# A hybrid pooling and windowed-attention layer on eight cores: pooling on GpSimd, gates in token layout, crossbar transposes

## The reference, cut to what matters

```python
h = modulate(rms_norm(x, g_pre), shift, scale)                 # tokens x 1024, 4096 tokens a sample
xa, ga, q, k, v, gb, gm = split_columns(h @ w_in)              # 512 512 1024 256 256 1024 2048 columns
# branch A: per group of 128 channels, window w = 2, 4, 8, 16
pooled = mean(xa[t - w/2 : t + w/2]) - xa[t]                   # valid positions only
y_a = (pooled @ pool_w[g]) * pool_scale * silu(ga)
# branch B: each token attends to +-128 tokens, 256 context keys and a sink; 16 heads, 4 kv heads, rotary q and k
y_b = attention(q, k, v, k_ctx, v_ctx, sink) * silu(gb)
g = sigmoid(gm)
merged = g[:, :1024] * (y_a @ w_branch_a) + g[:, 1024:] * (y_b @ w_branch_b)
out = x + gate * rms_norm(merged @ w_out, g_post)
```

## Time and profile before

| | |
|---|---|
| time, median of 3 runs | 2472.1 us (2468.12 to 2604.85) |
| span of the profiled execution, slowest core | 2465.5 us |
| spans of the eight cores | 2454.4 to 2465.5 us |
| mean granted TensorE clock, by core | 0.989 to 0.992 |
| DMA, mean share of the 16 engines busy | about 0.15 after the first 200 us |

### The profile page before, as it was taken

One profiled execution on the slowest core, in us unless ns is written; L12 is line 12 of the kernel. 1 busy time (PEld: TensorE's weight loads), 2 busy tenths in 40 slices (PEclk: granted clock), 3 DMA queues, 4 the chain that ended last, 5 costly groups with the idle time before them and its releaser, 6 DMA issues.

```text
span 2465.5 us, 85698 instructions; the slowest of 8 cores (2454.4 to 2465.5 us)
## 1 busy us (share of the span) xinstructions
PE 2367.6 (96%) x34464; PEld 1821.1 (74%) x34464; DVE 1341.5 (54%) x3567; ACT 1225.7 (50%) x2375; POOL 678.0 (28%) x677
## 2 busy tenths in 40 slices
PE   6679999999999999999999999999999999999998
PEld 2447877787787787778777778777777877777776
DVE  1425555555555655555555555565555556556553
ACT  1324555555555555455544555555555555555453
POOL 1112232232323223223222232322322323232232
PEclk9889999999999999999999999999999999999999
DMA  8982111111111111111112111111111111111111
GB/s 220 188 157 66 49 49 55 40 58 47 41 58 49 47 49 49 56 40 61 61 40 66 47 40 58 49 48 48 49 56 40 58 47 40 58 49 49 39 39 44
DMA packets 44371, 148.35 MB, mean 60 GB/s; under 512 B 7376, under 2 KB 15696, under 8 KB 41424
## 3 DMA queue, kind: packets, MB, share of 16 engines
q1 hardware_dynamic: 41392, 121.18, 15.1%
q0 software_dynamic: 2592, 21.69, 5.0%
HBM read 126.79 MB, written 33.56 MB: 65 GB/s over the span
## 4 chain that ended last, share of the span: by engine, by line
PE 88%; DVE 3%; DMA 2%; POOL 2%; issue 2%; ACT 2%; another core or an unknown queue 1%; POOLq 0%; DVEq 0%; SPq 0%; ACTq 0%
PE pb L483 34%; PE pb L476 13%; PE pb L692 9%; PE pb L708 9%; PE pb L642 6%; PE pb L616 6%; PE pb L682 5%; DVE s_scr L723 2%; DMA s_W<-w_in 2%; PE pb L578 2%; ACT s_ttmp L711 2%; PE tb L659 1%; POOL s_small L718 1%; PE pb L340 1%; PE tb L460 1%
## 5 line engine op out<-in xcount | busy, mean ns | idle before, releaser
L483 PEld LDWEIGHTS pb<-s_hT,s_W 128*128 128x128 bf16 x15360 | 866.5, 98 | 145.9 <-issue 145.3
L483 PE MATMUL pb<-s_hT,s_W 128*128 128x128 bf16 x15360 | 937.2, 219 | 22.1 <-DVE s_scr L723 21.3
L619 ACT ACTIVATE s_PT<-pb 128x512 bf16<-128x512 f32 x1264 | 651.8, 603 | 271.9 <-PE pb L616 271.8
L476 PE MATMUL pb<-s_W,s_hT 128*128 128x512 bf16 (+1 forms) x2048 | 421.3, 354 | 2.4 <-DMA s_W<-w_in 2.4
L535 DVE TENSOR_TENSOR s_scr<-pb,s_ropet 128x512 f32<-128x512 f32 x256 | 164.9, 686 | 311.0 <-PE pb L483 310.7
L476 PEld LDWEIGHTS pb<-s_W,s_hT 128*128 128x128 bf16 x2048 | 192.8, 98 | 160.0 <-issue 6.0
L540 POOL TENSOR_TENSOR s_qT<-s_scr 128x512 bf16<-128x512 f32 x128 | 160.0, 1271 | 539.8 <-DVE s_scr L535 539.8
L696 POOL TENSOR_TENSOR s_mgT<-s_ub,s_scr 128x512 bf16<-128x512 f32 x128 | 162.4, 1269 | 404.8 <-DVE s_scr L673 404.8
L692 PE MATMUL pb<-s_ybT,s_wmf 128*128 128x128 bf16 x4096 | 249.6, 219 | 0.0
L651 DVE SCALAR_TENSOR_TENSOR s_yb<-pb,s_small,s_Gb 128x64 bf16<-128x64 f32 x1024 | 220.0, 277 | 29.1 <-DVE s_small L648 2.2
L708 PE MATMUL pb<-s_wmf,s_mgT 128*128 128x512 bf16 x1024 | 231.6, 379 | 1.5 <-POOL s_mgT L696 1.5
(11 more groups left out here) (78 smaller groups left out, 2248.3 us busy)
## 6 DMA issues: line engine op xcount, KB each, us to landing
s_xt<-x SPq DMA_DIRECT2D x64, 512.0 KB, 3.8
s_xr<-x SPq DMA_DIRECT2D x64, 512.0 KB, 3.8
y<-s_xr SPq DMA_DIRECT2D x64, 512.0 KB, 2.7
s_W<-w_in POOLq DMA_DIRECT2D x11, 1024.0 KB, 41.6
s_wmf<-w_mod SPq DMA_DIRECT2D x4, 2048.0 KB, 11.9
s_ropet<-rope SPq DMA_DIRECT2D x64, 128.0 KB, 2.1
s_wmf<-w_mod POOLq DMA_DIRECT2D x2, 2048.0 KB, 81.9
s_xt<-ctx SPq DMA_DIRECT2D x4, 512.0 KB, 11.0
```

Of the source, the lines that this page charges most:

```text
L476: E("pe", lambda e, k=k: e.matmul(out=pb[:, c0:c0 + n], lhsT=h[:, k, :], rhs=W[:, wblk, k, c0:c0 + n], start=(k == 0), stop=(k == 7)), rea ...
L483: E("pe", lambda e, c=c, k=k: e.matmul(out=pb[:, c * 128:(c + 1) * 128], lhsT=W[:, wblk, k, c * 128:(c + 1) * 128], rhs=h[:, k, :], start= ...
L619: E("act", lambda e, g=g: e.activation(out=PT[:, jb, g, :], in_=banks[g][0][:, :], func=AF.Exp, scale=0.125), reads=[banks[g][1]], writes= ...
```

## The change

1. Pooling leaves TensorE. `fold_pool` multiplies, once at the start, the `xa` columns of the input weight by `pool_w * pool_scale / -w` (32 matmuls, eight copies out of PSUM). `P_xa` now computes the folded product in feature layout into a ring `xp`. `pool1` is four dependent additions on GpSimd (568, 420, 272 and 128 fp32 elements a partition) that form the windows of 2, 4, 8 and 16. `pool2` is four VectorE instructions of 128 elements and a product of 512.
2. `gm`, `A_mm` and `B_mm` go to token layout. Their sum `mg` must then be transposed into `mgT`.
3. The TensorE transposes become DMA transposes on SyncE's queue (`turn`): `xsb` to `hT` (`turn_lat`, with the modulation `mod_lat` done in place afterwards), `yb` to `ybT`, `mg` to `mgT`. The bank `tb` becomes an eighth `pb`. `hT` has four buffers in place of three.
4. The output stage is one tile later (`hasO`, tile p-2), between `A_mm` and the third visit; there is one more period at the end. The product with `gg` is taken straight from PSUM; the inverse root is applied later, by VectorE together with the residual, in place of two GpSimd additions.

```diff
         def norm_mod(dst, nm, j, also=False):
             for k in range(8):
-                E("dve", lambda e, k=k: e.tensor_scalar(out=dst[:, k, :], in0=tp[:, k * 128:(k + 1) * 128],
+                E("dve", lambda e, k=k: e.tensor_scalar(out=dst[:, k, :], in0=dst[:, k, :],
...
+        def turn(dst, src, rd, wr, sem):
+            E("sp", lambda e: e.dma_start(out=dst, in_=src, transpose=True), reads=rd, writes=wr, dma_sem=dsem(sem))
...
         def pool1(t):
...
+            add(av(0, 4, 0, 142), xpv(o - 8, 0, 4, 142), xpv(o - 7, 0, 4, 142), rd, [a])
+            add(bv(1, 3, 0, 140), av(1, 3, 0, 140), av(1, 3, 2, 140), [a], [b_])
+            add(av(2, 2, 0, 136), bv(2, 2, 0, 136), bv(2, 2, 4, 136), [b_], [a])
+            add(bv(3, 1, 0, 128), av(3, 1, 0, 128), av(3, 1, 8, 128), [a], [b_])
...
+        def pool2(t, res):
+            r = t % NR
             for g in range(4):
+                E("dve", lambda e, g=g: e.scalar_tensor_tensor(out=view(ya, g * 128, [[128, 1], [1, 128]]), in0=xpv(8 + r * 128, g, 1, 128),
+                                                               scalar=float(POOL_WINDOWS[g]), in1=res[g][0], op0=ALU.mult, op1=ALU.subtract),
+                  reads=[bf(f"xp{r}"), res[g][1]], writes=[bf(f"ya{g}")] + ([bf("ya")] if g == 0 else []))
+            E("dve", lambda e: e.tensor_tensor(out=ya[:], in0=ya[:], in1=Ga[:], op=ALU.mult),
...
         def A_mm(tm, rd):
             pa, pab = next_bank()
+            for k in range(4):
+                E("pe", lambda e, k=k: e.matmul(out=pa[:, :], lhsT=ya[:, k * 128:(k + 1) * 128], rhs=Wa[:, k, rd * 512:(rd + 1) * 512],
```

More of the change, by code:

```diff
@@ L232, in build_program @@
         NR = 4
-        NH = 3
+        NH = 4
         NS = 4
@@ L567, in pool1 @@
         def pool1(t):
-            i = t % NT
-            pb, pbb = next_bank()
-            for g in range(4):
[L571 to L580, removed]
-                      reads=[bf(f"xa{rs}"), bf("band")], writes=[pbb], inc=(g == 3 and ti == len(terms) - 1))
@@ L582, in pool1 @@
[L582 to L591 removed]
+            i, r = t % NT, t % NR
@@ L656, in do_ybT @@
         def do_ybT(t):
[L657 to L661 removed]
+            turn(ybT[:], yb[:], ALL_YB, [bf("ybT")], "d_tyb")
         tm_n = [0]
@@ L776, in period @@
             if hasG:
-                do_ybT(p - 1)
                 u = A_mm(tm, 0)
+            if hasO:
+                so = [out_mm(p - 2, nb_) for nb_ in range(2)]
+                out_stat(p - 2)
+                if (p - 1) % NT == 0 and p - 1 < TT:
+                    load_gg((p - 1) // NT)
+            vis()
             if hasP:
                 P_xa(p + 1)
+            if hasG:
+                tm = gm(p - 1, 8)
             vis()
+            if hasO:
+                out_evac(p - 2, so)
             if p in CP:
@@ L807, in period @@
                 u = A_mm(tm, 1)
+            if hasA:
+                res = pool1(p)
+            if nxt:
+                norm_front()
+                next_load()
+                turn_lat(p + 2)
+            if p in CP:
+                ctx_kv(*CP[p])
             if hasA:
@@ L829, in period @@
             if hasA:
-                pool2(p)
+                pool2(p, res)
+            if nxt:
+                mod_lat(p + 2)
             if p == 0:
                 start_gate()
-            if hasG:
-                obs = out_mm(p - 1)
-                out_evac(p - 1, obs)
-                if p % NT == 0 and p < TT:
-                    load_gg(p // NT)
         start_loads()
@@ L849, in build_program @@
             ctx_kv(0, j)
-        T_lat(0)
-        for p in range(-1, TT + 1):
+        turn_lat(0)
+        mod_lat(0)
+        norm_front()
+        next_load()
+        turn_lat(1)
+        fold_pool()
+        mod_lat(1)
+        for p in range(-1, TT + 2):
             period(p)
```

253 lines of the change are left out of this document (134 added, 119 removed).

## The result

The changed kernel takes 2726.5 us (median of five runs); the kernel before beside it took 2472.1. The ratio is 1.1005 (95% interval 1.0966 to 1.1043): 10% slower, nearly twice the loss that was forecast. Two of the five runs (2886.6 and 3072.2 us) had one die at a mean granted clock of 0.78 to 0.85 beside 0.92 on the other; such runs, and in one experiment the cores of such a die, are left out of every comparison. The other three took 2709.4, 2715.5 and 2726.5, so the kernel lies at the upper end of the stated range (2710) or up to 16 us above it. The profiled execution took 2715.5 us, its span is 2713.9, against 2465.5 before.

A forecast was written before the change was run, and what follows sets the result against it. TensorE, busy 96% of the span, was taken to bound the kernel. Terms: -139.5 (work removed) - 21 (bank wait) + 223 (wait) + 74 (clock) - 3 (startup and end) = +133 us, so 2605 us, +5.4%; range 2480 to 2710.

The forecast's parts named there:

- What leaves TensorE: TensorE's steady period: layouts save a net 0.38 us, transposes, band and `Wp` matmuls 1.80; together 2.18 us, 139.5 us in all.
- the bank wait: TensorE's wait for a PSUM bank, 0.33 us a period, 21 us in all, forecast to go.
- the cover: TensorE work between `gb` and the visit, 3.55 us of `out_mm`, which hid VectorE's work before and is now gone.
- The wait: TensorE before `P_kv`, waiting for VectorE's `pool2` and `mod_lat`: about 3.6 us (2.7 to 4.8) in 62 periods, 223 us.
- The clock: TensorE's clock falls after the 3 us idle gap: three times in four at 1.6 us, 1.2 a period, 74 us.
- Rival 1: TensorE before `P_kv`: the wait is there but the clock stays up; 2531 us (2475 to 2606), chance 0.20.
- Startup and end: Startup some 5 us earlier without `band` in the queue; end +2 for an extra transpose less two GpSimd additions; net -3.
- rival 2: DMA transposes land over 7 us after issue, VectorE waits for `hT` in 62 periods; 2853 us at 11 us; chance 0.14.
- the 7 us: SyncE's DMA transposes: the longest landing time allowed for one, at which it is hidden.
- Rivals 3 and 4: rival 3, and: long matmuls hide weight loads, so the layout brings 9.3 us a period net; 2035 us, chance 0.01.
- rival 3: VectorE's tail before `P_kv` is short, so the change is faster; decided at a 1.8 us wait, 2421 us; chance 0.12.
- GpSimd's additions: `pool1` on GpSimd: 4.1 us a period, hidden beside other work; 1 us slower would still be free.

## Why the prediction was right or wrong

**What leaves TensorE: right.** 2.18 us a period and the bank wait; with the cover given back, 33.74 us a period are measured for 33.69.

**The wait: right in place, cause and size.** Forecast 3.6 us a period, measured 3.88 (2.72 idle, 1.16 paced). Its terms: `pool2` 1.34 us instead of 1.6; the modulation 1.87 instead of 1.1, its instructions 0.23 apart, nearly those from PSUM (0.25 by the earlier trace rows), where I had taken 0.14. I chose the lower end because both operands were in SBUF; the upper end was the right one. In all the wait was 0.28 x 62, some 17 us, longer.

**The clock: right in kind, too small.** Forecast 1.2 us a period, from three gaps in four at 1.6 us; measured 1.74, and it fell behind both gaps shown. The earlier trace rows gave windows of 3.40 us at about half clock; in every second period the steady state shows 7.05 us at 0.55. This is 0.54 x 62, 33 us. Rival 1 falls: in the kernel after the clock does not stay up.

**Startup and end: the step that failed.** It said -3 us; the startup alone cost 45, and the end 7.5 beyond an ordinary period's loss. I set the transposes' landing by a load in the steady state (3.8 us) and let it stand for all of them. Four stand in the startup, where the bulk loads fill the DMA engines, and there the first took 58 us. At the end, an extra transpose and two additions less were to cost 2 us; nothing stood beside that transpose, and TensorE waited 5.6 us for it. The two context tiles inside the run were not priced at all: 17.6 us, 12 more than two ordinary periods lose. TensorE's row there:

```profile
1260.21 0.44 PE L501 MATMUL pb<-s_yb,s_W 128*128 128x128 bf16 x2 [2.82 <-DVE s_yb L473]
```

Waits of this kind, whose VectorE work itself waited for the transpose, make 3.3 us of the 8.5 by which that period is longer than the mean; the context's own matmuls are 1.8, and the clock, which falls behind this gap too (0.89 over the whole period), makes some 2.6. This is rival 2 after all, but in the startup, at up to 58 us for one tile, not in 62 periods at one or two. In the steady state the 7 us held: the three kinds of transpose land in 3.2 to 5.1 us. The list of DMA issues after (median us from issue to landing):

```profile
s_xt<-x SPq DMA_DIRECT2D x64, 512.0 KB, 4.5
...
s_hT<-s_xsb SPq DMA_TRANSPOSE x64, 5.1
s_ybT<-s_yb SPq DMA_TRANSPOSE x64, 4.6
...
s_mgT<-s_mg SPq DMA_TRANSPOSE x64, 3.2
s_yb<-s_xsb SPq DMA_TRANSPOSE x4, 17.1
```

**The baseline.** I took 36.49 us for the steady period, but that window reached 0.29 us past the next period's start; it is 36.20. The sum was made of differences, so it doesn't suffer. Two roundings (0.38 for a layout gain whose parts add up to 0.39, 4.8 for an upper end of the wait that comes to 4.7) change nothing either. By its terms the change was to be -2.18 - 0.33 + 3.6 + 1.2 = +2.3 a period; it was +3.02.

Summed up: +133 forecast, +248 measured between the spans. Startup and end 56, context tiles 12, clock 33 and wait 17 make 118 for the missing 115. The wait and the clock alone, with their misses, would have left the time near 2655 us, inside the range; the startup, the end and the context tiles took it to the edge and over. Rivals 3 and 4 fall: the wait is at 3.9 us a period, above rival 3's 1.8, and the layouts brought what the earlier trace rows say. GpSimd's additions took 3.5 us in all (4.1 forecast); no wait of TensorE, and no difference of the steady period with one of them doubled, shows any of it. What the prediction left unsaid is that the loss is one of order only: with `P_kv` a few calls later, `gm 8` ahead of visit 3 and the startup's transposes on TensorE, the same change is 5.4% faster than the kernel before.

## What to carry to other kernels

When work leaves a full engine, look for what it covered: count, on each other engine's list, what stands between the last thing it was given and the first thing the full engine reads back, and move that read, not the work. Do it for each result of the tail separately, since a swap that frees one reader makes another wait. Price the clock too: filling the gap gave back 1.74 us a period, though it added work. A transfer's price in the steady state is not its price in the startup, beside the bulk loads, or at the end, where nothing hides it.

## What the runs showed of the hardware

- A gap of 1.38 us in each period, with TensorE otherwise nearly full, was enough for a mean clock of 0.95 and cost 1.37 us a period beyond itself; gaps of 2.72 us gave 0.93, while a single gap of 3.09 us in the startup was not followed by a fall. Filling the gap with matmuls that nobody reads gave back 1.74 us a period.
- A transposing DMA of 256 KB within SBUF lands in 3.2 to 5.1 us (medians) in the steady state, next to 2.7 to 4.5 for plain ones of 512 KB; beside the startup's bulk loads it took up to 58. The Trainium skill (Advanced Engine Details and Errata, "X-Bar Transpose (TRN2)") says that they are as fast as regular ones on trn2; by bytes, from issue to landing, they are slower here. They bring some 207,000 packets more, nearly all under 512 B, and each holds SyncE for 1.2 us or more.
- `tensor_scalar` on 128 bf16 elements in place in SBUF goes at 0.23 us, from PSUM at 0.25: at this size where the operand lay hardly mattered.
- The dependent additions on GpSimd were faster than the line through the earlier trace rows: 1.13, 0.89, 0.65 and 0.46 us for 568, 420, 272 and 128 elements.
